# Order of logarithms, exponentials and decay factors on ScalarE in the gated delta recurrence

## What is computed

```
w = -softplus(-(w0 + tanh(w_lo) @ w_decay_up)) - 0.5
kk = heads(k * k_k)
kk = kk / maximum(sqrt(sum(kk * kk, -1)), 1e-12)        # keys of length one
k = k * (1.0 + (a - 1.0) * k_a)
decay = exp(-exp(heads(w)))
# scan over the 512 tokens, S is 64 x 64 for each head
sa = S @ (-kk_t)
S = S * decay_t + outer(sa, kk_t * a_t) + outer(v_t, k_t)
y_t = S @ r_t
# behind the scan
y = (y - mean(y)) * rsqrt(var(y) + GN_EPS) * gn_gain + gn_bias
y = (y + sum(r * k * r_k) * v) * g
```

## Time and profile before

| What | Before |
|---|---|
| Time, median of 3 runs | 3586.97 us (3586.68 to 3587.43) |
| Profiled execution, its span | 3591.0 us |
| PE busy, share of the span | 3331.0 us, 93% |
| PEld busy | 2719.1 us, 76% |
| DVE busy | 2043.5 us, 57% |
| ACT busy | 946.8 us, 26% |
| POOL busy | 470.8 us, 13% |
| The recurrence, from the first load of its masks to the next stage | 1843.2 to 2168.3 us |

### The profile page before, as it was taken

How to read it: one execution, slowest core, us unless ns; L and a number is a source line. 1 busy time by engine, 2 the same in 40 slices (tenths; PEclk the granted TensorE clock), 3 DMA queues, 4 the chain that set the end, 5 groups by cost and what they waited for, 6 DMA issues and landing times. The chain is left out here.

```text
span 3591.0 us, 50869 instructions
## 1 busy us (share of the span) xinstructions
PE 3331.0 (93%) x21206; PEld 2719.1 (76%) x21206; DVE 2043.5 (57%) x2764; ACT 946.8 (26%) x1677; POOL 470.8 (13%) x369
## 2 busy tenths in 40 slices
PE   7999999999999999899979888999989789899998
PEld 6777788878778877688748886787868568688786
DVE  6555544553464454699856664424456565688734
ACT  2146200111432231222253441222110560100104
POOL 0000111010013552100034430000020000100001
PEclk9999999999999999999989999999999899999998
DMA  3211123232314543332200003222223202222222
GB/s 132 63 42 48 48 94 100 81 121 93 66 62 138 184 167 117 102 107 97 74 28 4 3 4 105 83 94 94 94 73 106 84 4 91 94 94 93 74 97 71
DMA packets 210404, 298.62 MB, mean 83 GB/s; under 512 B 32803, under 2 KB 111279, under 8 KB 210063
## 3 DMA queue, kind: packets, MB, share of 16 engines
q1 hardware_dynamic: 210190, 295.59, 24.8%
HBM read 291.25 MB, written 4.32 MB: 82 GB/s over the span
## 5 line engine op out<-in xcount | busy, mean ns | idle before, releaser
L457 PE MATMUL bank<-h_hi_cut,ring_hi_cut 128*128 128x512 f32 x1928 | 760.8, 395 | 37.5 <-PEq L745 12.8
L457 PE MATMUL bank<-h_hi_cut,ring_cut 128*128 128x512 f32 x1928 | 754.7, 391 | 0.0
L457 PE MATMUL bank<-h_cut,ring_hi_cut 128*128 128x512 f32 x1832 | 717.9, 392 | 0.0
L510 DVE CAST ring_hi_cut<-ring 128x4096 fp32r<-128x4096 f32 (+5 forms) x97 | 197.9, 2040 | 649.5 <-DMA ring<-in_ffn_w_gu 138.5
L457 PEld LDWEIGHTS bank<-h_hi_cut,ring_hi_cut 128*128 128x128 f32 x1928 | 364.4, 189 | 118.7 <-issue 29.5
L457 PEld LDWEIGHTS bank<-h_hi_cut,ring_cut 128*128 128x128 f32 x1928 | 364.1, 189 | 78.6
L457 PEld LDWEIGHTS bank<-h_cut,ring_hi_cut 128*128 128x128 f32 x1832 | 346.2, 189 | 74.5 <-issue 2.2
L512 DVE TENSOR_TENSOR ring_cut<-ring,ring_hi_cut 128x4096 fp32r<-128x4096 f32 (+5 forms) x97 | 380.6, 3923 | 7.3
L457 PE MATMUL bank<-hidden_cut,ring_hi_cut 128*128 128x512 f32 x848 | 325.6, 396 | 0.0
L457 PEld LDWEIGHTS bank<-hidden_cut,ring_hi_cut 128*128 128x128 f32 x848 | 160.3, 189 | 40.1 <-issue 1.2
L332 POOL TENSOR_TENSOR work<-work 128x512 f32<-128x512 f32 x35 | 52.7, 1505 | 1001.5 <-ACT work L316 1001.4
(11 more groups left out here) (633 smaller groups left out, 5998.2 us busy)
## 6 DMA issues: line engine op xcount, KB each, us to landing
ring<-in_ffn_w_gu SPq DMA_DIRECT2D x44, 1024.0 KB, 6.5
ring<-in_w_in SPq DMA_DIRECT2D x21, 2048.0 KB, 7.8
ada_w<-in_ada_w SPq DMA_DIRECT2D x12, 2048.0 KB, 8.1
ring<-in_w_up SPq DMA_DIRECT2D x22, 1024.0 KB, 6.4
ring<-in_w_ff_in SPq DMA_DIRECT2D x8, 2048.0 KB, 8.7
ring<-in_w_ff_out SPq DMA_DIRECT2D x8, 2048.0 KB, 7.9
ring<-in_ffn_w_down SPq DMA_DIRECT2D x8, 1536.0 KB, 6.6
ring<-in_w_out SPq DMA_DIRECT2D x6, 2048.0 KB, 7.8
```

The lines of the kernel that those rows point to most:

```text
L457: last = nc.tensor.matmul(to, lhs, rhs, start=st and q == 0, stop=sp_ and q == len(parts) - 1)
L510: dve.tensor_copy(high, whole)
```

## The change

On ScalarE alone, the order within a turn is rewritten. `key_roots` is cut into `key_logs` (the logarithm, with its wait for "ss") and a new `key_roots` (the exponential); `roots` is cut into `logs` (the logarithm, with its wait for "var") and a new `roots`. In a turn the logarithm of the keys now stands at level 1 behind `square_of_y`. At level 2 stand the logarithm of the variance, one drain, the two exponentials, and `growth`. The decay factors move from level 1 to level 0. Level 3 has only its two copies.

```diff
-                        def key_roots(t):
+                        def key_logs(t):
                             until(act, "ss", t)
                             act.activation(nrm, nrm, ACT.Ln)
-                            act.drain()
+
+                        def key_roots():
                             act.activation(nrm, nrm, ACT.Exp, scale=-0.5).then_inc(rk["rn"].sem, 1)
...
-                        def roots(t):
+                        def logs(t):
                             until(act, "var", t)
                             act.activation(var[:], var[:], ACT.Ln, bias=eps[:, 2:3], scale=1.0 / HD)
-                            act.drain()
+
+                        def roots():
                             act.activation(var[:], var[:], ACT.Exp, scale=-0.5).then_inc(rk["rstd"].sem, 1)
...
                                 if l == 0 and more:
                                     squares_of_keys(T + 1)
+                                    decay_factors(T + 1)
                                 if l == 1:
                                     if t >= 0:
                                         square_of_y(t)
                                     if more:
-                                        decay_factors(T + 1)
-                                if l == 2 and more:
-                                    growth(T + 1)
-                                    key_roots(T + 1)
-                                if l == 3 and t >= 0:
-                                    roots(t)
+                                        key_logs(T + 1)
+                                if l == 2:
+                                    if t >= 0:
+                                        logs(t)
+                                    act.drain()
+                                    if more:
+                                        key_roots()
+                                    if t >= 0:
+                                        roots()
+                                    if more:
+                                        growth(T + 1)
                             if not new:
                                 square_of_y(t)
-                                roots(t)
+                                logs(t)
+                                act.drain()
+                                roots()
```

More of the change, by code:

```diff
@@ L2019, in _ @@
                         growth(0)
-                        key_roots(0)
+                        key_logs(0)
+                        act.drain()
+                        key_roots()
                         for T in range(TURNS + 1):
```

## The result

| What | Before | After |
|---|---|---|
| Time, median of 4 runs | 3586.84 us (3586.68 to 3587.43) | 3613.10 us (3611.77 to 3615.54) |
| Ratio to before | | 1.0073, 95% interval 1.0059 to 1.0088 |
| Profiled execution, its span | 3591.0 us | 3610.5 us |
| Stage of the recurrence in the profile | 325.1 us | 350.2 us |
| ACT busy in the whole span | 946.8 us | 931.0 us |

The kernel is 26.3 us slower, more than twice the 12.1 us that were forecast, and its time lies just above the range. The stage runs from the first load of its masks (1843.2 us before, 1838.8 after) to the first transfer of the next stage (2168.3 and 2189.02), and grew by 25.1 us. ScalarE has its 12 table loads less (12 x 1.28 = 15.4 us of the 15.8 that it is less busy).

The account below looks back on a forecast made before the run. A turn is bound by its longest chain across engines, with `normed`'s start as clock hand. Six turns at 1.76 us (10.6), turn 0 +0.2 and turn 7 +1.3 made +12.1 us: 3599.1 us, 0.34% slower, range 3592 to 3612.

Parts of the forecast that it names:

- `normed` as the clock hand of a turn: Behind level 3, VectorE's `normed` start sets turn length; 1.76 us later in each of turns 1 to 6.
- The load of level 1 is hidden: Level 1's 1.28 us table load runs while the key logarithm waits for "ss"; level 2 is 1.20 us late.
- "var" is the wait that costs: At level 2 ScalarE idles for "var", then needs 2.82 us; level 3 starts 2.47 us late.
- Turns 0 and 7: Turn 0 +0.2 us; turn 7 has level 3 2.43 us late and `normed` +1.3 us.
- The decay factors cost nothing: Moved to level 0, their 0.62 us fits ScalarE's 1.76 us wait for "yc".
- The rule to do everything of one set before switching: Skill page's rule favouring the change: two table switches fewer per turn, each some 2.66 us with drain.
- the estimate of 32: By the skill page, two fewer switches in each of six turns would free 32 us of ScalarE.
- TensorE's clock as a rival at 14 in 100: Longer level 3 gaps bring more 1.2 GHz stretches; six more at 2.3 us add 14 us, 3613; 14 in 100.

Follow-up runs that it names:

- third and fourth experiments: Third: Pairs at level 2, 3593.24 us; fourth: Pairs across two levels, 3572.22 us.
- decay factors alone: Kernel before with only the decay factors moved from level 1 to level 0: 3588.29 us, ratio 1.0000.
- again: The changed kernel, unaltered, run once more beside other kernels: 3610.29 us, ratio 1.0059.
- Level 3 filled: Changed kernel with two extra bonus sums matmuls on TensorE in its level 3 wait: 3609.77 us, ratio 1.0062.
- Key logarithm alone: Against before: key logarithm at level 1, decay factors at level 0; growth, keys' exponential stay at level 2, variance operations at level 3: 3598.21 us.
- Pairs at level 2: Against the changed kernel: growth and key logarithm ahead of the variance logarithm at level 2, decay factors back at level 1: 3593.24 us, ratio 1.0017.
- Pairs across two levels: Against the changed kernel: growth, key logarithm at level 2; variance logarithm, both exponentials at level 3 behind its copies; decay factors at level 1: 3572.22 us.
- Both filled: Level 3 filled plus one extra bonus sums matmul behind level 2's products: 3602.58 us, ratio 1.0037.
- Before, level 3 filled: Kernel before with one extra bonus sums matmul in TensorE's level 3 wait: 3587.55 us, ratio 0.9998.

## Why the prediction was wrong

The time was wrong, the schedule right. By its own steps:

- *`normed` as the clock hand of a turn, 1.76 us later.* Right: the full-clock turn is 38.97 us, against 37.20, 1.77 more. Level 2 starts 1.21 us late (20.86 us into the turn, against 19.65) with TensorE's new wait of 1.04 (about 1.1 was said), the wait at level 3 is 2.24 us (2.3).
- *The load of level 1 is hidden.* Right: ScalarE waits 0.30 us behind it.
- *"var" is the wait that costs, 2.82 us of list behind it.* Right (2.80), and the third and fourth experiments show that it is the order around the waits and not the pairing that costs.
- *Turns 0 and 7.* Turn 7's level 3 starts 2160.01 - 2135.05 = 24.96 us into the turn, where it was 2140.54 - 2117.99 = 22.55: 2.41 late, against 2.43. But `normed` starts 29.24 us into the turn where it was 26.35, 2.89 late and not 1.3, since level 3's products run at the low clock (3.63 us for 2.01). Turn 0 has a low stretch in it, and its 0.2 us can't be read off.
- *The decay factors cost nothing.* Right.
- *The rule to do everything of one set before switching* (the Trainium skill, ScalarE: Activation LUTs, section "Rules for kernel authors"). It is right where the order lets it be: the kernel with the pairs across levels 2 and 3 follows it and gains. ScalarE's busy time fell by 15.8 us and not by the estimate of 32, which counts the drain that the Trainium skill adds in "What ACT_TABLE_LOAD costs" of the same page; the rows show none, the next load follows the logarithm's end by 0.05 us (1914.98 + 0.30 to 1915.33).
- **The step that failed: TensorE's clock as a rival at 14 in 100 and outside the sum.** The sum kept before's 3.5 us of low clock as they were. In the trace of before the stretch of turn 1 begins 3.1 us behind the start of the level 3 wait (1.00 us, ScalarE's late copy) and that of turn 2 begins 1.4 us behind the start of the level 4 wait (1.51 us, the late root). The forecast itself lengthened the first of these waits and added one at level 2, without a price for either. In turns 0 to 6 the clock took about 14.1 us, 10.6 more than before, and in the rest of the stage 2.4 more (3.66 less the 1.3 of schedule). 12.1 + 10.6 + 2.4 is 25.1, by which the stage grew. The rival's own working (six more stretches at 2.3 us, 14 us on top, 3613) met the measured 3613.1, and that is luck in part. Before, turn 2's stretch cost 2.35 us and turn 1's only 1.2, so 2.3 was one turn's price. In turns 0 to 6 four more turns have a stretch, and not six, and some cost more (3.6 us in turn 0). The rival also blamed the level 3 wait. The runs show that the new wait at level 2, which the rival did not name, is where most of the stretches begin: five of six and seven of seven in the changed kernel's two profiles, four of four with the level 3 wait filled, six of six with the level 3 wait gone, and none is left when both waits are filled.

The table has TensorE's waits at the levels in a full-clock turn, and the number of turns 0 to 6 with a low stretch, with the wait that it follows. Us throughout.

| Kernel | Level 2 | Level 3 | Level 4 | All idle time | Low stretches |
|---|---|---|---|---|---|
| Before; decay factors alone | 0 | 1.00 | 1.51 | 4.31 | 2 and 2 (each: 1 level 3, 1 level 4) |
| The change; again | 1.04 | 2.24 | 0.79 | 5.88 | 6 (5 level 2, 1 level 3); 7 (level 2) |
| Level 3 filled | 1.03 | 0.52 | 0.79 | 4.15 | 4 (level 2) |
| Key logarithm alone | 1.03 | 0 | 0.79 | 3.63 | 6 (level 2) |
| Pairs at level 2 | 0 | 1.72 | 0.79 | 4.32 | 3 (level 3) |
| Pairs across two levels | 0 | 0 | 0.79 | 2.60 | 0 |
| Both filled | 0 | 0.52 | 0.79 | 3.32 | 0 |
| Before, level 3 filled | 0 | 0 | 1.51 | 3.46 | 4 (level 4) |

What stays open: why a wait of about 1 us at level 2 is followed by a fall of the clock in most turns, and the same at level 3 in one turn of seven. The rows show where, not why. Also open is what makes a stretch long. With the level 3 wait filled those of the full turns were short, but the key logarithm alone has one of 17.2 us without that wait.

The profiled span grew by 19.5 us and the medians by 26.3. The profile of before is the slowest of all ahead of the stage: its turn 0 starts at 1861.03 us, that of the nine other profiles between 1852.74 and 1857.39. The stage grew by 25.1 us. Ahead of it the changed kernel's profile is 4.4 us shorter than that of before and behind it 1.2, in stages that the change does not touch; why executions differ there is not explained.

## What to carry to other kernels

Before an operation with a wait is moved ahead of the copies on which the busiest engine lives, read when the waited-for value is ready and what fills the time until then: the same pairing of logarithms and exponentials lost 26 us with ScalarE idle at two waits, and won 17 us where both halves stood one level later. Then read the granted clock turn by turn, take full-clock turns for the schedule, and put a price on every new wait of TensorE of about 1 us, for the clock as well. If such a wait can't be removed, fill it with harmless matmuls and see: with both waits of the changed kernel filled, it ran 7.7 us faster here. With one of the two waits of the kernel before filled, nothing was won.

## What the runs showed of the hardware

- A wait of 1.04 us on TensorE, between stretches of dense small matmuls, is followed by a stretch at 1.2 GHz in most turns (22 of 28 over four profiles with such a wait at level 2). In the changed kernel, where a second wait of 2.24 us comes 5.5 us later, full turns with such a stretch lose 1.3 to 2.7 us in one profile and 1.2 to 2.5 in the other (40.16 to 41.67 us against 38.97), with one exception that lost nothing; with the second wait filled, 0.62 us.
- Each of the 34 low stretches that the ten profiles show in turns 0 to 6 begins 1.0 to 3.3 us behind the start of a TensorE wait of 1.00 us or more, and none behind the waits of 0.79 us that every full-clock turn has. The reverse does not hold: before, the same wait of 1.00 us at level 3 stands in all seven turns, and the clock falls behind it in one.
- Three extra 128x512 matmuls in a turn, in the two waits (1.98 us for the two of level 3, 1.10 us for the one of level 2), took the changed kernel from 3610.29 to 3602.58 us on one chip.
- A table load issues while its activation still waits for its operand (1909.01 against 1910.59), and PSUM copies between two logarithms force no load (1974.85 to 1976.06 in the kernel with the pairs across two levels).
